# Expert layer of a two-block transformer: TensorE weighs a quad of tokens, and gives back its row places, two tiles sooner

## The chip, the cores and the metric

The kernel runs on one core of a Trainium2 chip. The time is that of one execution on the device, in microseconds (us); where several runs were made, it is their median. PE is TensorE, DVE is VectorE, ACT is ScalarE, POOL is GpSimd, SP is SyncE, whose queue issues the plain transfers.

## The reference

Two blocks follow each other on 256 tokens of width 1024: first two layers with attention or retention and a mixture of experts, then one layer that ends in `peer_ffn`. The change is in the last part alone:

```python
def peer_ffn(x, w_q, sub_k1, sub_k2, u_tab, v_tab):
    ...
    top_s, pos = lax.top_k(cand_s, PEER_TOPK)
    experts = jnp.take_along_axis(cand_i, pos, axis=-1)
    gates = jax.nn.softmax(top_s, axis=-1)
    ...
    def chunk(args):
        xc, ec, gc = args
        u = u_tab[ec].astype(f32)
        act = jax.nn.gelu(jnp.einsum('ced,cd->ce', u, xc.astype(f32))) * gc
        return jnp.einsum('ce,ced->cd', act, v_tab[ec].astype(f32)).astype(x.dtype)
```

Each token picks 128 of 16384 experts (8 heads, 16 each). An expert is a row `u` (a key, 1024 numbers) and a row `v` (a value). A token's output is the sum of its experts' values, each weighted by gelu(u.x) and its gate.

## The kernel before, in words

The stage `peer_stage` treats the 256 tokens in two halves, in two ways at once.

One half goes **by tiles**: all 16384 key rows are read in 128 tiles of 512 KB (`keys(n)`, n = 0 to 127), then all value rows in 128 more (`values(m)`, m = 0 to 127). SP's queue fetches them in this order into 6 places (and 13 spare ones for the first tiles); a place is fetched anew once PE has used the tile in it (`tile_used`).

The other half goes **by tokens**: POOL gathers the 128 rows of `u` and `v` that one token picked into one of 8 row places (1 MB each, `peer_rows_a`, `_b`, `_c`). A quad is four tokens. Two tokens make a pair p. `spread_pair(p)` on PE copies both tokens' x to all partitions (8 matmul rows); DVE's two `dot`s then multiply and sum; when a quad's four dots are done, ACT's `open_quad` applies the gelu and scales by the gates (four copies, semaphore `acted`). `values_of(q)`, called here the weighing of quad q, waits for `acted`, multiplies the four tokens' value rows (16 matmul rows at L3095) and signals `rows_used`. POOL waits for `rows_used` of quad q before it gathers the four tokens of quad q+2 into the places.

All of it shares the 16 DMA engines. PE, ACT, DVE and POOL each work in the order in which the code is written. That order has four parts: tiles 0 to 47, while DVE also picks the experts of the other half (`picks(0, ...)`, `recover(0, ...)`; the dots of pairs 0 to 7 stand between its steps; `PAIR_AT` says behind which tile a pair is spread: 19, 22, ... 40); then `turn_picks(0, 6)` and a wait for `selT_made`; then ten rounds of eight key tiles with three pairs each and, up to round eight, four gate units (L3107); then 128 value tiles with the remaining 26 pairs (`pairs_before`), one pair every four or five tiles. The end is a norm of both halves (from L3400) and the store.

Of the kernel before, what the change touches and what calls it, by code (L numbers as in the profile page):

```python
# [2859 lines left out]
PK = 128  # L2860
# [5 lines left out]
QUADS = P // QUAD  # L2866
# [10 lines left out]
PAIR_AT = {FIRST_TOKEN + 1 + 3 * p: p for p in range(BESIDE_PICKS // 2)}  # L2877
BESIDE_UNITS = 3 * GROUPS_LEFT
VALUES_FROM = BESIDE_PICKS + BESIDE_UNITS
# [81 lines left out]
def peer_stage(K, S, products, first, scores, room, out):  # L2961
# [28 lines left out]
    def pairs_before(m):  # L2990
        return VALUES_FROM // 2 + min(-(-m * ((TOKENS - VALUES_FROM) // 2) // (PK - 6)), (TOKENS - VALUES_FROM) // 2)

    with nc.Block() as block:  # L2993
# [22 lines left out]
        def _(pe):  # L3016
# [38 lines left out]
            def keys(n):  # L3055
                pe.wait_ge(tile_in[PLACE[n]], 16 * TURN[n])
                if n % 4 == 0 and n >= 8:
                    if n - 8 < EARLY:
                        pe.wait_ge(gelu_done, n // 4 - 1)
                    else:  # L3060
                        pe.wait_ge(tile_gated, (n - 8 - EARLY) // 4 + 1)
                u = first.slot(n).rearrange("p (k e) -> p k e", k=KD)
                for k in range(KD):
                    last = pe.matmul(K.bank[:, 2 + n // 4 % 2, n % 4 * P:(n % 4 + 1) * P], u[:, k, :], xT[:, k, :], start=(k == 0),  # L3064
                                     stop=(k == KD - 1))
                last.then_inc(tile_used, 1)
# [7 lines left out]
            def spread_pair(p):  # L3074
                if p:
                    pe.wait_ge(dotted, 2 * p)
                else:
                    pe.wait_ge(index_made, 1)
                for dh in range(2):
                    for n, part in enumerate(first.x_rows):  # L3080
                        for r in range(2):
                            t, own = token(2 * p + r), slice(64 * r, 64 * (r + 1))
                            last = pe.matmul(K.bank[:, 4 + 2 * r + dh, :], first.ident[own, t:t + 1].to_broadcast([64, P]),  # L3083
                                             part[own, dh * 512:(dh + 1) * 512], start=(n == 0), stop=(n == 1))
                last.then_inc(spread, 1)

            def weigh_pair(p):
                if p % 2 == 0 and p:
                    values_of(p // 2 - 1)

            def values_of(q):
                pe.wait_ge(acted, QUAD * (q + 1))
                for dh in range(2):
                    for g in range(QUAD):
                        last = pe.matmul(K.bank[32 * strip(g):32 * (strip(g) + 1), dh, :], W[:, q % 2, g, 31 - q:63 - q],  # L3095
                                         rows[(QUAD * q + g) % ROWS_HELD][:, D + dh * 512:D + (dh + 1) * 512], start=(q == 0),
                                         stop=(q == QUADS - 1))
                last.then_inc(rows_used, 1)

            def gate_unit(m):  # L3100
                pe.wait_ge(a_ready, m + 1)
                pe.wait_ge(b_ready, m + 1)
                pe.wait_ge(dotted, BESIDE_PICKS + 2 * (3 * (m // 4) + m % 4 // 2 + 1))
                if m >= 2:
                    pe.wait_ge(h_gated, m - 1)
                for q in range(QT):
                    last = pe.matmul(K.bank[:, 6 + m % 2, q * P:(q + 1) * P], a_hot[:, m % 2, q, :], b_hot[:, m % 2, q, :],  # L3107
                                     start=True, stop=True)
                last.then_inc(g_made, 1)

            def values(m):
                n = PK + m
                pe.wait_ge(tile_in[PLACE[n]], 16 * TURN[n])
                for dh in range(2):
                    last = pe.matmul(K.bank[:, 2 + dh, :], H[:, m, :], first.slot(n)[:, dh * 512:(dh + 1) * 512], start=(m == 0),  # L3115
                                     stop=(m == PK - 1))
                last.then_inc(tile_used, 1)
# [4 lines left out]
            for n in range(FIRST_TILES, EARLY):  # L3122
                keys(n)
                if n in PAIR_AT:
                    spread_pair(PAIR_AT[n])
                if n - 1 in PAIR_AT:
                    weigh_pair(PAIR_AT[n - 1])
            pe.wait_ge(dotted, BESIDE_PICKS)
            turn_picks(0, 6)
            pe.wait_ge(selT_made, 1)  # L3130
            for e in range(GROUPS_LEFT // 2):
                n, m, p = EARLY + 8 * e, 4 * e, BESIDE_PICKS // 2 + 3 * e
                spread_pair(p)
                keys(n)
                weigh_pair(p)
                keys(n + 1)
                if m < UNITS:
                    gate_unit(m)
                    gate_unit(m + 1)
                keys(n + 2)  # L3140
                pe.wait_ge(h_gated, min(m + 2, UNITS))
                spread_pair(p + 1)
                keys(n + 3)
                weigh_pair(p + 1)
                keys(n + 4)
                if m < UNITS:
                    gate_unit(m + 2)
                    gate_unit(m + 3)
                keys(n + 5)
                pe.wait_ge(h_gated, min(m + 4, UNITS))  # L3150
                spread_pair(p + 2)
                keys(n + 6)
                weigh_pair(p + 2)
                keys(n + 7)
            pe.wait_ge(h_gated, UNITS)
            pe.wait_ge(tile_gated, GROUPS_LEFT)
            for m in range(PK):
                for p in range(pairs_before(m), pairs_before(m + 1)):
                    spread_pair(p)
                values(m)  # L3160
                for p in range(pairs_before(m), pairs_before(m + 1)):
                    weigh_pair(p)
                if m == PK - 5:
                    values_of(QUADS - 1)

        @block.gpsimd
        def _(pool):
# [426 lines left out]
```

## Time and profile before

| | us |
|---|---|
| median of 3 runs (lowest, highest) | 1901.48 (1900.75, 1904.99) |
| the profiled execution, its time | 1908.66 |
| its span in the trace | 1906.8 |
| PE busy, share of the span | 1772.8, 93% |
| DVE, ACT, POOL busy | 905.9, 433.7, 431.5 |

Busy times of the whole span mix stages with different limits. The stage in question begins its key tiles at about 1228 us and takes the rest of the span. What ends a wait in each of its parts is told by the chain of work that ended last and by the GB/s that the DMA engines moved.

### The profile page before, as it was taken

To read this page: it belongs to the slowest core of one execution; us is meant where nothing else is said; L and a number is where in the kernel's file an instruction comes from. 1 tells how busy PE (TensorE), PEld (TensorE's weight loads), DVE (VectorE), ACT (ScalarE), POOL (GpSimd) and SP (SyncE) were. 2 spreads that over 40 slices of the span, in tenths; PEclk is the share of its full clock that TensorE was granted. 3 is DMA by queue.
4 is the path that set the end of the run, shared out by engine and by line. 5 is a ranking of instruction groups with operands and counts; after the bars stand their busy time and mean duration, and the time that the engine had idled before them with its cause. 6 is when DMAs were issued, how large, how long until landed. Compare 5 with 4: busy or idle time off the path is not lost. (4 is left out here: it accounts for less than half of the span.)

```text
span 1906.8 us, 23745 instructions
## 1 busy us (share of the span) xinstructions
PE 1772.8 (93%) x9356; PEld 1136.8 (60%) x9356; DVE 905.9 (48%) x1978; ACT 433.7 (23%) x847; POOL 431.5 (23%) x312
## 2 busy tenths in 40 slices
PE   4989999988999999998899999999999997999998
PEld 4975444436887754442586656988888874333333
DVE  4467311114477842111598743988776642211222
ACT  5462211114345321110330324311011110000001
POOL 5820000006667600000110004314222221121110
PEclk8999899998999989999999999999999999999999
DMA  9986899995567769999632335398999999999996
GB/s 395 354 324 213 326 430 429 429 430 194 198 245 286 270 253 429 430 428 429 259 122 99 120 131 218 133 383 333 402 414 415 415 416 410 388 407 403 403 401 248
DMA packets 95089, 620.29 MB, mean 325 GB/s; under 512 B 11520, under 2 KB 12032, under 8 KB 60672
## 3 DMA queue, kind: packets, MB, share of 16 engines
q1 hardware_dynamic: 75824, 482.88, 63.5%
q0 software_dynamic: 18432, 134.23, 17.3%
q8 instruction: 78, 1.28, 0.3%
q10 hardware_dynamic: 720, 1.61, 0.2%
q14 instruction: 35, 0.29, 0.0%
HBM read 617.63 MB, written 1.05 MB: 324 GB/s over the span
## 5 line engine op out<-in xcount | busy, mean ns | idle before, releaser
L3115 PE MATMUL bank<-peer_tiles_a,peer_H 128*128 128x512 f32 x344 | 159.7, 604 | 16.7 <-DMA peer_tiles_a<-in_peer_v 16.7
L232 POOL TENSOR_TENSOR w_lo<-ring,w_hi 128x1024 fp32r<-128x1024 f32 x60 | 148.1, 2471 | 64.5 <-ACT w_hi L222 64.1
L3322 DVE CUSTOM_DVE_ANT_0 peer_junk<-peer_rows_b,bank 128x1024 bf16<-128x1024 f32 x64 | 76.8, 1217 | 146.0 <-issue 138.7
L1096 PE MATMUL bank<-ring,moe_slots 128*64 128x512 f32 x576 | 131.4, 607 | 9.8 <-DMA ring<-in_stream 9.8
L3064 PEld LDWEIGHTS bank<-peer_xT,peer_tiles_a 128*128 128x128 f32 x1104 | 127.3, 192 | 21.4 <-issue 15.6
L3064 PE MATMUL bank<-peer_xT,peer_tiles_a 128*128 128x128 f32 x1104 | 135.2, 278 | 4.7 <-DMA peer_tiles_a<-in_peer_u 4.7
L3322 DVE CUSTOM_DVE_ANT_0 peer_junk<-peer_rows_a,bank 128x1024 bf16<-128x1024 f32 x48 | 57.4, 1218 | 146.7 <-issue 131.9
L3115 PEld LDWEIGHTS bank<-peer_tiles_a,peer_H 128*128 128x128 f32 x344 | 62.1, 189 | 105.5 <-issue 73.5
L3179 POOL DMA_INDIRECT peer_rows_b<-in_peer_uv,peer_index x64 | 60.0, 937 | 235.3 <-PE bank L3095 220.4
L3179 POOL DMA_INDIRECT peer_rows_a<-in_peer_uv,peer_index x48 | 48.2, 1003 | 264.5 <-PE bank L3095 218.6
L1277 DVE TENSOR_TENSOR bank<-bank,mod 128x512 f32<-128x512 f32 x32 | 22.4, 700 | 175.3 <-PE bank L1146 175.3
L1096 PE MATMUL bank<-early,moe_slots 128*64 128x512 f32 x448 | 102.0, 597 | 3.6 <-DMA early<-in_stream 3.6
L1146 PE MATMUL bank<-ring,moe_hidT 128*64 128x512 f32 x448 | 99.8, 595 | 3.8 <-issue 2.3
L339 DVE CUSTOM_DVE_ANT_0 mod<-sb_mod_ring,bank 128x1024 bf16<-128x1024 f32 x64 | 76.6, 1217 | 47.3 <-DMA sb_mod_ring<-in_ada_t 22.9
L1096 PEld LDWEIGHTS bank<-ring,moe_slots 128*64 128x64 f32 x576 | 43.0, 139 | 93.2 <-issue 76.1
L3221 ACT ACTIVATE peer_opened<-peer_pre 128x4 f32<-128x4 f32 x32 | 6.6, 206 | 386.6 <-DVE peer_pre L3322 377.5
L222 ACT ACTIVATE w_hi<-ring 128x1024 fp32r<-128x1024 f32 x60 | 63.6, 1060 | 108.8 <-PE bank L261 73.1
L3115 PE MATMUL bank<-peer_tiles_b,peer_H 128*128 128x512 f32 x168 | 79.2, 605 | 4.2 <-DMA peer_tiles_b<-in_peer_v 4.1
L3064 PEld LDWEIGHTS bank<-peer_xT,peer_tiles_b 128*128 128x128 f32 x544 | 64.8, 196 | 14.0 <-issue 12.7
L3064 PE MATMUL bank<-peer_xT,peer_tiles_b 128*128 128x128 f32 x544 | 70.2, 284 | 3.1 <-issue 2.9
L1465 POOL TENSOR_TENSOR w_lo<-ring,w_hi 128x1024 fp32r<-128x1024 f32 x4 | 9.5, 2417 | 280.6 <-ACT w_hi L1205 280.6
L1146 PEld LDWEIGHTS bank<-ring,moe_hidT 128*64 128x64 f32 x448 | 32.6, 137 | 63.7 <-issue 56.1
(515 smaller groups left out, 3684.0 us busy)
## 6 DMA issues: line engine op xcount, KB each, us to landing
ring<-in_stream SPq DMA_DIRECT2D x103, 2048.0 KB, 12.8
early<-in_stream SPq DMA_DIRECT2D x32, 2048.0 KB, 18.4
peer_tiles_a<-in_peer_v SPq DMA_DIRECT2D x86, 512.0 KB
peer_tiles_a<-in_peer_u SPq DMA_DIRECT2D x69, 512.0 KB
sb_mod_ring<-in_ada_t SPq DMA_DIRECT2D x64, 512.0 KB, 6.3
peer_tiles_b<-in_peer_v SPq DMA_DIRECT2D x42, 512.0 KB
peer_tiles_b<-in_peer_u SPq DMA_DIRECT2D x34, 512.0 KB
ret_mod_ring<-in_ada_t SPq DMA_DIRECT2D x32, 512.0 KB, 5.0
```

Of the source, the lines that this page charges most:

```text
L222: act.activation(self.shaped(self.w_hi, q, by_columns), self.quarter(n, q, by_columns), ACT.Copy).then_inc(self.hi_made, 1)
L232: pool.tensor_tensor(self.shaped(self.w_lo, q, by_columns), self.quarter(n, q, by_columns), self.shaped(self.w_hi, q, by_columns).bitcast( ...
L339: dve.tensor_tensor_reduce(out=self.junk[:, b % 2, :], in0=self.ring[:, b % self.slots, :], in1=c_wide, scale=1.0, scalar=0.0, op0=ALU.mul ...
L1096: last = pe.matmul(K.bank[own(e), 4 + up, :], slots[:, f, own(2 * p + e)], w[:, e, k, :], start=(f == 0), stop=(f == KD - 1))
L1146: last = pe.matmul(K.bank[own(e), 6 + dh, :], hidT[:, k, own(e)], w[:, e, k, :], start=(k == 0), stop=(k == 3))
L1277: dve.tensor_tensor(y, y, K.mod[:, 2 * D + dh * 512:2 * D + (dh + 1) * 512], ALU.mult).then_inc(y_gated, 1)
L1465: pool.tensor_tensor(next_shaped(w_lo, q), next_quarter(q), next_shaped(w_hi, q).bitcast(F32), ALU.subtract).then_inc(next_lo, 1)
L3064: last = pe.matmul(K.bank[:, 2 + n // 4 % 2, n % 4 * P:(n % 4 + 1) * P], u[:, k, :], xT[:, k, :], start=(k == 0), stop=(k == KD - 1))
L3115: last = pe.matmul(K.bank[:, 2 + dh, :], H[:, m, :], first.slot(n)[:, dh * 512:(dh + 1) * 512], start=(m == 0), stop=(m == PK - 1))
L3179: pool.indirect_dma_start(rows[i % ROWS_HELD], None, K.A["peer_uv"], bass.IndirectOffsetOnAxis(ap=index[:, token(i):token(i) + 1], axis=0) ...
L3221: act.activation(opened[:, q % 2, :], pre[:, q, :], ACT.Gelu_apprx_tanh).then_inc(quad_gelu, 1)
L3322: dve.tensor_tensor_reduce(out=junk[:, i % 2, :], in0=rows[i % ROWS_HELD][:, 0:D], in1=wide_row(i % 2), scale=1.0, scalar=0.0, op0=ALU.mul ...
```

## The change

A pair's call of `weigh_pair` now weighs the quad that the pair itself ends (p odd), where it weighed the quad ended by the pair before (p even). The calls stand elsewhere: in the first part two tiles behind the spread of the odd pair; in the rounds behind the gate units that follow two tiles later; among the value tiles behind the fourth tile from the spread, `weigh_pair(VALUES_FROM // 2 - 1)` behind the first one.

```diff
             def weigh_pair(p):
-                if p % 2 == 0 and p:
-                    values_of(p // 2 - 1)
+                if p % 2:
+                    values_of(p // 2)
...
-                if n - 1 in PAIR_AT:
-                    weigh_pair(PAIR_AT[n - 1])
+                if n - 2 in PAIR_AT:
+                    weigh_pair(PAIR_AT[n - 2])
...
                 spread_pair(p)
                 keys(n)
-                weigh_pair(p)
+                if e:
+                    weigh_pair(p - 1)
                 keys(n + 1)
                 if m < UNITS:
                     gate_unit(m)
                     gate_unit(m + 1)
+                weigh_pair(p)
                 keys(n + 2)
...
                 keys(n + 3)
-                weigh_pair(p + 1)
                 keys(n + 4)
                 if m < UNITS:
                     gate_unit(m + 2)
                     gate_unit(m + 3)
+                weigh_pair(p + 1)
                 keys(n + 5)
...
                 keys(n + 6)
-                weigh_pair(p + 2)
                 keys(n + 7)
...
                 values(m)
-                for p in range(pairs_before(m), pairs_before(m + 1)):
-                    weigh_pair(p)
-                if m == PK - 5:
-                    values_of(QUADS - 1)
+                if m == 0:
+                    weigh_pair(VALUES_FROM // 2 - 1)
+                if m >= 3:
+                    for p in range(pairs_before(m - 3), pairs_before(m - 2)):
+                        weigh_pair(p)
```

Three places of PE's order are shown. A key tile is 8 matmuls (L3064), a value tile 2 (L3115), a spread the four rows of L3083, a weighing the four rows of L3095.

**PE, first part, tiles 35 to 40, with the weighing of quad 2.** Before, from tile 35:

```order
L3064 MATMUL bank<-peer_xT,peer_tiles_b 128x128 x16
L3064 MATMUL bank<-peer_xT,peer_tiles_a 128x128 x8
L3083 MATMUL bank<-peer_x_rows_hi,peer_ident 128x512 x2
L3083 MATMUL bank<-peer_x_rows_lo,peer_ident 128x512 x2
L3083 MATMUL bank<-peer_x_rows_hi,peer_ident 128x512 x2
L3083 MATMUL bank<-peer_x_rows_lo,peer_ident 128x512 x2
L3064 MATMUL bank<-peer_xT,peer_tiles_a 128x128 x8
L3095 MATMUL bank<-peer_rows_a,peer_W 32x512 x3
L3095 MATMUL bank<-peer_rows_b,peer_W 32x512
L3095 MATMUL bank<-peer_rows_a,peer_W 32x512 x3
L3095 MATMUL bank<-peer_rows_b,peer_W 32x512
L3064 MATMUL bank<-peer_xT,peer_tiles_a 128x128 x16
```

With the change, from the same tile 35:

```order
L3064 MATMUL bank<-peer_xT,peer_tiles_b 128x128 x16
L3095 MATMUL bank<-peer_rows_a,peer_W 32x512 x3
L3095 MATMUL bank<-peer_rows_b,peer_W 32x512
L3095 MATMUL bank<-peer_rows_a,peer_W 32x512 x3
L3095 MATMUL bank<-peer_rows_b,peer_W 32x512
L3064 MATMUL bank<-peer_xT,peer_tiles_a 128x128 x8
L3083 MATMUL bank<-peer_x_rows_hi,peer_ident 128x512 x2
L3083 MATMUL bank<-peer_x_rows_lo,peer_ident 128x512 x2
L3083 MATMUL bank<-peer_x_rows_hi,peer_ident 128x512 x2
L3083 MATMUL bank<-peer_x_rows_lo,peer_ident 128x512 x2
L3064 MATMUL bank<-peer_xT,peer_tiles_a 128x128 x24
```

The weighing stood behind tile 38; it stands behind tile 36, ahead of tile 37 and ahead of the spread of pair 6.

**PE, end of the first part, with the weighing of quad 3.** Before, from tile 43 on (the 3 transposes of L3071 are `turn_picks`):

```order
L3064 MATMUL bank<-peer_xT,peer_tiles_a 128x128 x32
L3064 MATMUL bank<-peer_xT,peer_tiles_b 128x128 x8
L3071 MATMUL bank<-consts,peer_sel 128x128 x3
L3083 MATMUL bank<-peer_x_rows_hi,peer_ident 128x512 x2
L3083 MATMUL bank<-peer_x_rows_lo,peer_ident 128x512 x2
L3083 MATMUL bank<-peer_x_rows_hi,peer_ident 128x512 x2
L3083 MATMUL bank<-peer_x_rows_lo,peer_ident 128x512 x2
L3064 MATMUL bank<-peer_xT,peer_tiles_b 128x128 x8
L3095 MATMUL bank<-peer_rows_b,peer_W 32x512 x3
L3095 MATMUL bank<-peer_rows_c,peer_W 32x512
L3095 MATMUL bank<-peer_rows_b,peer_W 32x512 x3
L3095 MATMUL bank<-peer_rows_c,peer_W 32x512
```

With the change, from tile 41 on:

```order
L3064 MATMUL bank<-peer_xT,peer_tiles_b 128x128 x16
L3095 MATMUL bank<-peer_rows_b,peer_W 32x512 x3
L3095 MATMUL bank<-peer_rows_c,peer_W 32x512
L3095 MATMUL bank<-peer_rows_b,peer_W 32x512 x3
L3095 MATMUL bank<-peer_rows_c,peer_W 32x512
L3064 MATMUL bank<-peer_xT,peer_tiles_a 128x128 x32
L3064 MATMUL bank<-peer_xT,peer_tiles_b 128x128 x8
L3071 MATMUL bank<-consts,peer_sel 128x128 x3
L3083 MATMUL bank<-peer_x_rows_hi,peer_ident 128x512 x2
L3083 MATMUL bank<-peer_x_rows_lo,peer_ident 128x512 x2
L3083 MATMUL bank<-peer_x_rows_hi,peer_ident 128x512 x2
L3083 MATMUL bank<-peer_x_rows_lo,peer_ident 128x512 x2
```

The weighing stood behind tile 48, past the transposes and the spread of pair 8; it stands behind tile 42, ahead of tiles 43 to 47 and of the transposes.

**PE, the last value tiles, with the weighing of quad 31.** Before, from tile 117 on:

```order
L3115 MATMUL bank<-peer_tiles_b,peer_H 128x512 x4
L3115 MATMUL bank<-peer_tiles_a,peer_H 128x512 x8
L3115 MATMUL bank<-peer_tiles_b,peer_H 128x512 x2
L3095 MATMUL bank<-peer_rows_b,peer_W 32x512 x3
L3095 MATMUL bank<-peer_rows_c,peer_W 32x512
L3095 MATMUL bank<-peer_rows_b,peer_W 32x512 x3
L3095 MATMUL bank<-peer_rows_c,peer_W 32x512
L3115 MATMUL bank<-peer_tiles_b,peer_H 128x512 x2
L3115 MATMUL bank<-peer_tiles_a,peer_H 128x512 x6
```

With the change, also from tile 117 on:

```order
L3115 MATMUL bank<-peer_tiles_b,peer_H 128x512 x4
L3115 MATMUL bank<-peer_tiles_a,peer_H 128x512 x4
L3095 MATMUL bank<-peer_rows_b,peer_W 32x512 x3
L3095 MATMUL bank<-peer_rows_c,peer_W 32x512
L3095 MATMUL bank<-peer_rows_b,peer_W 32x512 x3
L3095 MATMUL bank<-peer_rows_c,peer_W 32x512
L3115 MATMUL bank<-peer_tiles_a,peer_H 128x512 x4
L3115 MATMUL bank<-peer_tiles_b,peer_H 128x512 x4
L3115 MATMUL bank<-peer_tiles_a,peer_H 128x512 x6
```

Four value tiles stood behind the last weighing; seven do. In the same way quad 29, the last whose places are gathered anew, was weighed behind value tile 103 and is weighed behind tile 101; quad 19 behind tile 9, and now 7.

## Rows read from the trace of the kernel before

**Rows 1.** The page: span, and DMA share in 40 slices.

```profile
span 1906.8 us, 23745 instructions
...
DMA  9986899995567769999632335398999999999996
```

**Rows 2.** Stretches of the stage: engines busy, granted clock, DMA share, GB/s.

```profile
core 0: us, PE busy (x) PEld busy (x) DVE busy (x) ACT busy (x) POOL busy (x), PEclk, DMA share, GB/s
1288.00:1308.00 20.00, 20.00 (x172) 16.16 (x165) 17.64 (x78) 2.25 (x7) 5.97 (x7) 1.00 0.66 246
1308.00:1328.00 20.00, 20.00 (x168) 16.73 (x167) 17.24 (x33) 5.01 (x10) 16.68 (x7) 1.00 0.98 387
...
1364.00:1372.00 8.00, 8.00 (x70) 7.43 (x69) 3.66 (x6) 1.64 (x6) 3.45 (x4) 1.00 0.92 350
1372.00:1618.00 246.00, 231.35 (x1812) 182.40 (x1811) 137.29 (x287) 24.95 (x88) 52.49 (x56) 1.00 1.02 415
1618.00:1630.00 12.00, 12.00 (x46) 4.77 (x45) 2.37 (x4) 0.00 (x0) 3.76 (x4) 1.00 0.82 285
1630.00:1848.00 218.00, 204.35 (x671) 82.33 (x673) 47.18 (x79) 10.56 (x50) 33.76 (x36) 1.00 1.01 408
```

**Rows 3.** Chain that ended last, around the first row places of values.

```profile
1597.66 17.54 DMA peer_tiles_a<-in_peer_v
...
1615.25 3.70 PE bank L3115 x8
1618.95 1.13 PE bank L3083 x8
1620.07 1.91 PE bank L3115 x4
1621.99 1.85 PE bank L3095 x16
```

**Rows 4.** The same chain, near its end.

```profile
1847.64 1.86 PE bank L3095 x16
...
1899.90 1.23 DVE x L3400
```

**Rows 5.** One value tile in PE's order of time, with its wait.

```profile
1866.71 1.98 PE L3115 MATMUL bank<-peer_tiles_b,peer_H 128*128 128x512 f32 x4 [0.66 <-DMA peer_tiles_b<-in_peer_v]
```

**Rows 6.** Instructions of PE in order of time, while picks are made.

```profile
1309.70 3.84 PE L3064 MATMUL bank<-peer_xT,peer_tiles_b 128*128 128x128 f32 x32
...
1315.25 0.49 PE L3083 MATMUL bank<-peer_x_rows_hi,peer_ident 64*128 64x512 f32 x2
...
1318.35 0.63 PE L3095 MATMUL bank<-peer_rows_a,peer_W 128*32 128x512 f32 x3
...
1328.77 7.31 PE L3064 MATMUL bank<-peer_xT,peer_tiles_a 128*128 128x128 f32 x64
...
1338.20 0.49 PE L3071 MATMUL bank<-consts,peer_sel 128*128 128x128 f32 x3
1339.34 0.50 PE L3083 MATMUL bank<-peer_x_rows_hi,peer_ident 64*128 64x512 f32 x2 [0.65 <-DVE peer_selT L3373]
...
1342.43 0.63 PE L3095 MATMUL bank<-peer_rows_b,peer_W 128*32 128x512 f32 x3
...
1354.64 2.02 PE L3107 MATMUL bank<-peer_scores 128*128 128x128 f32 x16
...
1361.49 0.63 PE L3095 MATMUL bank<-peer_rows_a,peer_W 128*32 128x512 f32 x3
```

**Rows 7.** Instructions of DVE in the same stretch.

```profile
1311.07 1.22 DVE L3322 CUSTOM_DVE_ANT_0 peer_junk<-peer_rows_a,bank 128x1024 bf16<-128x1024 f32 x1 [1.55 <-PE bank L3083]
...
1316.69 1.22 DVE L3322 CUSTOM_DVE_ANT_0 peer_junk<-peer_rows_b,bank 128x1024 bf16<-128x1024 f32 x1 [0.87 <-PE bank L3083]
```

**Rows 8.** Instructions of ACT in the same stretch.

```profile
1313.71 0.85 ACT L3229 ACTIVATE peer_W<-peer_opened,peer_gates 128x1 f32<-128x1 f32 x4
...
1329.87 0.85 ACT L3229 ACTIVATE peer_W<-peer_opened,peer_gates 128x1 f32<-128x1 f32 x4
```

## The prediction

> **What bounds the kernel now.** I read the page first: the 16 DMA engines are at 9 tenths in nearly every slice of the last third, with one gap before it [rows 1]. Then I cut the stage into stretches [rows 2]. From 1372 to 1618 us the DMA engines move 415 GB/s at a share of 1.02, while PE has 231.35 of 246 us busy: PE waits 14.7 us there, the DMA engines never. From 1630 to 1848 it is 408 GB/s. Here bytes decide. But there are holes: 246 GB/s from 1288 to 1308, 387 up to 1328, 350 around 1364 and 285 from 1618 to 1630. Against 415 these are 8.1, 1.3, 1.3 and 3.8 us of lost transfer time (length times the missing share). In a hole all 6 tile places are full or wait for PE, and the row places wait for a weighing. So three things decide in turn: the order on PE, DVE and ACT up to about 1364, then the DMA engines, and at the very end PE alone: from quad 29's weighing at 1847.64 to the last tile's end at 1899.90, 52.3 us [rows 4], PE waits only once, 0.66 us before the tile at 1866.71 [rows 5].
>
> A tile (512 KB) costs the DMA engines 1.26 us at 415 GB/s, a quad's gathers (4 x 1 MB) 10.1 us. On PE a key tile costs 1.83 us (four in 7.31 [rows 6]), a value tile 1.8 (two in 3.70, with a switch), a spread 1.13 and a weighing 1.85 [rows 3].
>
> **The change part by part.** No instruction is added or removed; most of the 32 weighings move. What counts is what stands behind each on PE (tiles, spreads, transposes) and on POOL (the gathers), and whether the wait for ACT's copies still has cover.
>
> *The first part: a new wait.* Before, quad 2 was weighed at 1318.35, while ACT's copies ended at 1313.71 + 0.85 = 1314.56: cover of 3.8 us. Quad 3 was weighed at 1342.43 against copies that ended at 1330.72: 11.7 us [rows 6, 8]. With the change this cover goes. The spread of pair 5 ends at 1309.70, where tile 35 starts; tiles 35 and 36 take 3.7 and end at 1313.4; the copies come at 1314.56: PE waits 1.2 us, weighs for 1.85, does tile 37 (1.9) and only then spreads pair 6 (1.13), which ends at 1319.5. It was spread at 1315.25, and its dot began at 1316.69, held by PE for the last 0.87 [rows 6, 7]. The dot now begins at about 1319.8, 3.1 us late. Quads 0 and 1 are moved likewise; by the same sum they make the spread of pair 5 itself 0.5 to 1.4 us late (estimate). So DVE is 3.4 to 4.5 us late from pair 6 on, and nothing between that dot and quad 3's copies waited for anybody else: the copies end at 1334.1 to 1335.2.
>
> PE has by then fallen less behind: tile 42 ends at about 1330.3 (it was 1328.77, where tile 43 starts). It waits about 4 us, weighs (1.85), and does tiles 43 to 47 (9.4 to the transposes before, 9.2 without the small wait in it): transposes at 1345.2 to 1346.3 for 1338.20. The spread of pair 8 followed them by 1.14 [rows 6]: now at 1346.3 to 1347.4, 7.0 to 8.1 late. A weighing (1.85) no longer follows, but the first gate unit, which waits for pair 8's dots, had that as cover; I take 0.6 us for it (estimate). PE comes to tile 49, and so to what follows, 7.0 - 1.85 + 0.6 = 5.8 to 8.1 - 1.85 + 0.6 = 6.9 us late. Queued behind the wait: tiles 43 to 47, so their places, so SP's next fetches.
>
> *What it gives back there.* Quad 4 is weighed behind the gate units that end at 1354.64 + 1.86 = 1356.5 instead of at 1361.49 [rows 6]. Late by the above that is 1362.3 to 1363.4 for a start; it was 1361.49. So the request for quad 6's rows comes 0.8 to 1.9 us later than before, I take the middle, **+1.4**, and at that moment PE has done two tiles fewer (52 for 54), so two fewer places were fetched anew: a debt of 2 x 1.26 = **+2.5 us** of transfer. Its other side is a bigger hole around 1364. From here to the value tiles the DMA engines decide, PE's 14.7 us of waiting absorb its own delay, and in the rounds the weighings that move keep their cover: two tiles and two gate units (3.7 + 1.86 = 5.5 us) lie between the spread's end and them, and from the end of pair 5's spread to its copies' end it was 1314.56 - 1309.70 = 4.9.
>
> *Quad 18 to quad 19.* Quad 18 keeps its place. Quad 19 was weighed at 1621.99 behind tile 9; it is now weighed behind tile 7, which arrives at 1615.25 and is done at 1617.1: 4.9 us sooner [rows 3]. Two tiles less are 2.5 us of transfer, and the hole of 3.8 us [rows 2] gives the rest: **-4.9**. From quad 19 to quad 29 there are 94 tiles before and after, with as many long gaps of ten tiles, and a burst of gathers stands alike to the tiles around it. So the small holes in 408 GB/s come again: **0**.
>
> *The end.* Behind quad 29's weighing stand two more value tiles (3.6) and the spread of pair 60 (1.13); the wait of 0.66 may vanish. PE decides there, so this is paid in full: +4.0 to +4.7, I take **+4.4**. The last weighing, three tiles sooner, gives nothing: what follows it waits for the last tile [rows 4].
>
> **Sum:** 1.4 + 2.5 - 4.9 + 4.4 = **+3.4 us**. The profiled execution took 1908.66 us for a span of 1906.8, 7.2 above the median; I put the difference onto both: 1912.1 in such a run, 1901.48 + 3.4 = **1904.9** as a median.
>
> *A rule against this sum.* The row shows one rate, 415 GB/s, with gathers and tiles in flight together [rows 2]. The Trainium skill, DMA: Bandwidth & Descriptors, section Issuing engines are not separate DMA queues, says that transfers from any engine end up on the same 16 DMA engines and interleave. By that rule an earlier request only changes whose bytes go first: the sum would be 0 and the time 1901.5. By the rows it is +3.4, as PE, not the DMA engines, holds both ends. The rate agrees with the rule in the middle.
>
> **The rivals.**
> - *Faster: the new wait costs nothing.* If DVE's late pair 6 is caught up (its steps to the next dots may have slack that the records do not show), +1.4 and +2.5 go. Earlier gathers of quads 2 to 5 then fill holes of the first stretch, up to 2.5 us of the 10.7 lost before 1372. 4.4 - 4.9 - 2.5 = -3.0: 1898.5. It decides once PE's waits for quads 2 and 3 together stay under 2 us. Against it: the copies of quad 3 lie 2 us behind tile 42 even with DVE's old times. Chance 0.2.
> - *Slower: the hole at 1618 only moves.* Tile 7 arrived with its neighbours in a bunch; if the gathers that come 4.9 us sooner meet them, the tiles behind are held up and quad 20 gains just the two tiles, 2.5. Then 1.4 + 2.5 - 2.5 + 4.4 = +5.8: 1907.3. For it: PE waited through a tile's 17.54 us there [rows 3]. Against it: 3.8 us in which little moved. Chance 0.2.
> - *No change: bytes alone decide.* The wait in the first part is paid from PE's 14.7 us and the end from tiles that come sooner: 1901.5, as by the rule above. Against it: the holes at both ends. Chance 0.15.
>
> **How the numbers follow.** The forecast keeps 0.45 with a range of its own of 1902.5 to 1907.5 (+0.8 or +1.9 for the first term, 4.0 or 4.7 for the last, and 1 us for rounding of holes). With the rivals' 1898.5 and 1907.3 and 1 to 1.5 us beside them for the median's own scatter, the range is 1897.5 to 1909. A measurement tells about 0.2%, 3.8 us, from no change: below 1897.7 lies half of the first rival and little else, 0.13; above 1905.3 lie nearly half of the forecast and most of the second, 0.38; the rest, 0.49, is the same within it.
>
> **What the profile after would show.** Right: PE waiting for ACT's copies ahead of L3095, 1 us for quad 2 and 3 to 5 us for quad 3; the transposes of the first part near 1345; a hole of 3 to 5 us near 1360 to 1366; none near 1618 and quad 19 weighed some 5 us sooner after quad 18; 56 to 57 us from quad 29's weighing to the last tile. Wrong: quad 3's weighing behind tile 42 with a wait under 1 us, or GB/s after 1372 that differ from 415 in the middle, since then the order of requests itself matters.

## The result: 6 us slower, about twice the forecast

| | before | after |
|---|---|---|
| median of 20 runs (lowest, highest) | 1903.02 us (1899.24, 1907.19) | 1908.97 us (1905.54, 1914.02) |
| ratio to before, 95% interval | | 1.0033 (1.0025 to 1.0042) |
| the profiled execution, its time | 1908.66 | 1910.28 |
| its span | 1906.8 | 1908.4 |

By the ratio the change costs 6.3 us (4.8 to 8.0) where the forecast had 3.4, and the sign is beyond doubt. The two profiled executions are only 1.6 us apart. The first thing to settle is therefore which of them stands for its kernel, and the trace of before does not. The page of after, against [rows 1]:

```profile
span 1908.4 us, 23745 instructions
...
DMA  9986899995568769999633335399899999999996
...
PE 24%; DMA 10%; DVE 3%; issue 1%; ACT 0%; DVEq 0%
```

It tells little: the same number of instructions, four of the 40 digits changed by one, and for the chain of work that ended last shares of PE and DMA only (the last line). So I read PE in order of time where the first waits were forecast. With [rows 6] beside it (in these rows a key tile is x16, a value tile x4 and a weighing x16):

```profile
1308.63 0.63 PE L3095 MATMUL bank<-peer_rows_a,peer_W 128*32 128x512 f32 x3 [0.16 <-ACT peer_W L3231]
...
1320.26 3.84 PE L3064 MATMUL bank<-peer_xT,peer_tiles_b 128*128 128x128 f32 x32
1327.96 1.08 PE L3095 MATMUL bank<-peer_rows_b,peer_W 128*32 128x512 f32 x3 [3.86 <-ACT peer_W L3231]
...
1331.54 8.55 PE L3064 MATMUL bank<-peer_xT,peer_tiles_a 128*128 128x128 f32 x64
...
1341.71 0.49 PE L3071 MATMUL bank<-consts,peer_sel 128*128 128x128 f32 x3
...
1348.61 1.58 PE L3107 MATMUL bank<-peer_scores 128*128 128x128 f32 x12 [0.78 <-DVE peer_pre L3324]
```

In front of quad 3's weighing PE stands still for 3.86 us, for ACT's copies. In front of quad 2's it is 0.16 us only, where I had 1.2. What I had not forecast comes behind the wait. One matmul of the weighing lasts 1.08 us instead of 0.63, the whole weighing takes 1331.54 - 1327.96 = 3.6 us instead of 1.85, and tiles 43 to 46 take 8.55 instead of 7.31. ACT's copies, as in [rows 8], end at 1327.06 + 0.85 = 1327.91:

```profile
1327.06 0.85 ACT L3231 ACTIVATE peer_W<-peer_opened,peer_gates 128x1 f32<-128x1 f32 x4
```

The stretches of after, with those of [rows 2] to compare (the last three columns are the granted clock, the DMA share and GB/s):

```profile
1272.00:1372.00 100.00, 94.20 (x761) 78.07 (x760) 77.96 (x213) 13.68 (x40) 28.07 (x21) 0.97 0.92 365
1324.00:1328.00 4.00, 0.14 (x5) 0.04 (x6) 3.97 (x6) 1.05 (x5) 0.00 (x0) 0.89 1.02 427
1328.00:1332.00 4.00, 4.00 (x18) 1.03 (x19) 3.93 (x3) 0.00 (x0) 0.09 (x1) 0.50 0.89 361
1332.00:1336.00 4.00, 4.00 (x29) 4.00 (x29) 2.42 (x4) 0.60 (x1) 3.08 (x4) 0.76 0.62 198
1350.00:1364.00 14.00, 14.00 (x118) 11.37 (x116) 11.92 (x29) 1.64 (x6) 2.36 (x2) 1.00 0.63 216
1372.00:1590.00 218.00, 211.22 (x1751) 175.20 (x1750) 133.48 (x280) 23.87 (x86) 53.12 (x52) 1.00 1.02 414
1618.00:1630.00 12.00, 7.82 (x16) 2.59 (x16) 2.17 (x4) 0.00 (x0) 1.61 (x2) 1.00 1.02 419
1630.00:1660.00 30.00, 26.82 (x89) 11.30 (x89) 7.11 (x12) 2.12 (x10) 3.74 (x4) 1.00 0.97 373
```

The granted clock is 0.50 from 1328 to 1332, the lower of the two levels (1.2 GHz), right behind 3.86 us in which PE did nothing. It is back at 1.00 (2.4 GHz) from 1336. The Trainium skill, TensorE: Matmul & The Clock Gate, section The HAM clock gate, says that the array falls to half its clock when it idles and gets it back once it is busy; the trace agrees. Two holes, stretches in which the DMA engines move much less than 415 GB/s, are seen in the last column: 198 GB/s from 1332 to 1336 and 216 from 1350 to 1364. From 1372 to 1590 it is 414, as before. The hole at 1618 is gone; one stands at 1630 to 1660.

The chain of work that ended last, near the end of after (start, us, what), as in [rows 4]:

```profile
1830.65 11.81 DMA peer_tiles_a<-in_peer_v
...
1844.49 1.85 PE bank L3095 x16
...
1853.04 10.52 DMA peer_tiles_a<-in_peer_v
...
1887.44 1.85 PE bank L3095 x16
1889.30 12.23 PE bank L3115 x28
1901.53 0.02 issue
1901.55 1.23 DVE x L3402
```

From quad 29's weighing it is 1901.53 - 1844.49 = 57.0 us to the last tile's end, with the seven tiles (12.23 us) behind the last weighing.

### The profile page after: what moved, and what is told of

It is laid out like the page before. It is cut to its first block and busy times, and to the rows that moved or that the text cites. A ratio compares the mean times of both kernels' runs of the same rounds, so it can differ in the third digit from the quotient of the medians.

```text
span 1908.4 us, 23745 instructions
## 1 busy us (share of the span) xinstructions
PE 1772.5 (93%) x9356; PEld 1136.5 (60%) x9356; DVE 908.3 (48%) x1978; ACT 433.1 (23%) x847; POOL 433.5 (23%) x312
## 5 line engine op out<-in xcount | busy, mean ns | idle before, releaser
L3115 PE MATMUL bank<-peer_tiles_a,peer_H 128*128 128x512 f32 x344 | 160.0, 604 | 17.2 <-DMA peer_tiles_a<-in_peer_v 17.2
L3064 PEld LDWEIGHTS bank<-peer_xT,peer_tiles_a 128*128 128x128 f32 x1104 | 128.2, 193 | 23.2 <-issue 16.1
L3064 PE MATMUL bank<-peer_xT,peer_tiles_a 128*128 128x128 f32 x1104 | 136.0, 280 | 4.9 <-DMA peer_tiles_a<-in_peer_u 4.9
L3115 PEld LDWEIGHTS bank<-peer_tiles_a,peer_H 128*128 128x128 f32 x344 | 62.1, 189 | 105.8 <-issue 73.9
L3115 PE MATMUL bank<-peer_tiles_b,peer_H 128*128 128x512 f32 x168 | 78.6, 603 | 2.5 <-DMA peer_tiles_b<-in_peer_v 2.5
L3064 PEld LDWEIGHTS bank<-peer_xT,peer_tiles_b 128*128 128x128 f32 x544 | 62.8, 192 | 11.9 <-issue 8.2
L3064 PE MATMUL bank<-peer_xT,peer_tiles_b 128*128 128x128 f32 x544 | 67.1, 279 | 2.7 <-DMA peer_tiles_b<-in_peer_u 2.7
## 6 DMA issues: line engine op xcount, KB each, us to landing
peer_tiles_a<-in_peer_u SPq DMA_DIRECT2D x69, 512.0 KB, 11.1
```

## The experiments

All kernels below but the one with a filler have the instructions of before. Where a weighing stands is written in tables, "behind tile n: quad q", so the line numbers differ a little (the weighing is L3093, a key tile L3066, a value tile L3113). Each ratio is to the kernel before on the same chip, in rounds; us are the ratio's distance from 1 times 1903. Intervals are 95%. Each kernel has one profiled execution, so what is read from traces rests on one execution each.

### The order of before, profiled once more

No edit but the tables with the old places (the second table, for the value tiles, is left out here):

```diff
+WEIGHED_FIRST = {26: 0, 32: 1, 38: 2}
```

> The order of before, profiled once more, since the profiled execution of before took 1908.66 us against a median of 1903.02 over 20 runs. Theory A (that execution lost some 5.5 us to a hiccup of PE ahead of the spread of pair 0, where PE's clock was 0.69 for 4 us, and everything behind it is late by that): a span near 1901, the spread of pair 0 some 5 us sooner, near 1265.5 as in the profile after. Theory B (the hiccup belongs to the order): it is there again, span near 1906.

It took 1903.1 us (span 1901.3), 5.6 less than the profiled execution of before. Nearly the whole difference lies ahead of pair 0's spread. In the trace of before, single matmuls of one tile stand apart there:

```profile
1261.62 0.36 PE L3064 MATMUL bank<-peer_xT,peer_tiles_b 128*128 128x128 f32 x1 [0.71 <-issue]
1262.33 0.27 PE L3064 MATMUL bank<-peer_xT,peer_tiles_b 128*128 128x128 f32 x1 [0.35 <-issue]
...
1264.46 4.90 PE L3064 MATMUL bank<-peer_xT,peer_tiles_b 128*128 128x128 f32 x27 [0.43 <-issue]
```

and as a stretch of the same kernel, the granted clock at 0.69:

```profile
1264.00:1268.00 4.00, 3.56 (x22) 3.54 (x22) 1.64 (x8) 0.60 (x1) 0.00 (x0) 0.69 1.03 431
```

Pair 0 is spread at 1271.08 in that execution and at 1265.92 in this one, 5.2 us sooner. So this trace, not the first, is the one to hold beside after; it is called "the order of before" from here on. Its stretches:

```profile
1272.00:1372.00 100.00, 99.17 (x829) 83.96 (x832) 84.04 (x229) 14.54 (x43) 30.17 (x21) 1.00 0.97 390
1350.00:1364.00 14.00, 14.00 (x118) 11.32 (x117) 9.47 (x21) 1.02 (x4) 3.75 (x4) 1.00 0.95 375
1372.00:1590.00 218.00, 210.98 (x1734) 172.44 (x1727) 130.25 (x270) 23.52 (x83) 48.97 (x53) 1.00 1.02 415
1618.00:1630.00 12.00, 12.00 (x36) 5.26 (x33) 2.37 (x4) 0.81 (x5) 3.76 (x4) 1.00 0.88 338
```

The loss of transfer time against 415 GB/s from 1272 to 1372 is 100 x (1 - 390/415) = 6.0 us here and 100 x (1 - 365/415) = 12.0 in after: 6.0 more, about the 6.3 of the ratio. (With the stretch laid from 20 to 120 us behind the first transposes of the picks in each execution, the rates change by 1 GB/s at most.)

### One part of the change at a time

```diff
 first: only the first part new
+WEIGHED_FIRST = {24: 0, 30: 1, 36: 2, 42: 3}
 rounds: only the rounds new (weighings behind the gate units)
 values: only the value tiles new
-WEIGHED_LAST = {0: 18, 9: 19, 18: 20, ... 93: 28, 103: 29, 112: 30, 123: 31}
+WEIGHED_LAST = {0: 18, 7: 19, 17: 20, ... 92: 28, 101: 29, 110: 30, 120: 31}
```

> Only the first part has the new order (quads 0 to 3 weighed behind tiles 24, 30, 36, 42); rounds and value tiles as before. Theory A (the first part holds the cost: PE's waits for ACT's copies, 3.9 us for quad 3 alone, and the slower clock behind that wait): slower by 4 to 7 us, ratio 1.002 to 1.004. Rival (the end holds it, the two tiles behind quad 29): within 1.5 us of before.

Measured: 1.0035 (1.0021 to 1.0049), +6.7 us (4.0 to 9.3). The first part alone costs what the whole change costs.

> Only the ten rounds have the new order; the first part and the value tiles as before. Theory A: the weighings keep their cover, quad 4 comes some 4.7 us sooner, the small hole near 1364 closes: 0 to 1.3 us faster, ratio 0.9993 to 1.0. Rival (requests that come sooner crowd out the tiles): slower by 1 to 3 us.

Measured: 0.9991 (0.9979 to 1.0002), -1.7 us (-4.0 to +0.4): a gain is not shown.

> Only the value tiles have the new order; first part and rounds as before. Theory A: quad 19 comes 4.9 us sooner and the end pays 4.8 us: within 1.5 us of before. Rival (the end holds the cost and the hole near 1618 only moves): slower by 3 to 5 us, ratio 1.0015 to 1.0026.

Measured: 0.9995 (0.9983 to 1.0006), -1.0 us (-3.2 to +1.1), where my sum had -4.9 + 4.4 = -0.5.

> The changed order in the rounds and among the value tiles, the first part as before. Theory A (the whole cost is in the first part): not slower, between -4 and 0 us against before, ratio 0.998 to 1.0. Rival (the later parts' own costs, the end above all, show once they are together): slower by 2 us or more.

Rounds and value tiles new, the first part old: 1.0001 (0.9993 to 1.0010), +0.2 us (-1.3 to +1.9). The whole change less this one is 6.3 - 0.2 = 6.1 us: the first part again.

### The first part: which quad, and the clock

```diff
 quads 0 to 2 only
+WEIGHED_FIRST = {24: 0, 30: 1, 36: 2}
 quad 3 only
+WEIGHED_FIRST = {26: 0, 32: 1, 38: 2, 42: 3}
```

> The order of before, but quads 0, 1 and 2 weighed behind tiles 24, 30 and 36, so ahead of the next pair's spread; quad 3 stays behind tile 48. Theory A (the cost of the first part is quad 3's wait of 3.9 us, with PE's slower clock behind it, on top of a DVE chain made some 3 us late by the spread of pair 6): transposes of the first part some 2.5 to 3 us late, no lower clock behind them, slower by 1 to 3 us, ratio 1.0005 to 1.0016. Rival (the late DVE chain alone is the cost): slower by 5 us or more.

Measured: 1.0007 (0.9997 to 1.0017), +1.3 us (-0.6 to +3.2). The clock stays at 1.00.

> The order of before, but quad 3 weighed behind tile 42 and not behind tile 48; quads 0 to 2 as before. Theory A: in the profile before, tile 42 ended 2 us ahead of the copies, so PE waits 2 us there and not 3.9; the transposes come 3.9 to 4.5 us late (2.0 of wait, 1.85 of weighing), of which 1.85 is given back behind the spread of pair 8: slower by 2 to 3 us, up to 5 if the clock falls behind this shorter wait too. Rival (quad 5's rows, asked for 9 us sooner, pay for it): same or faster.

Measured: 1.0000 (0.9990 to 1.0010), 0.0 us (-1.9 to +1.9), where 2 to 3 were expected. PE waits there too, but 1.69 us, and the clock stays up (the weighing takes 1.85 again):

```profile
1322.88 0.63 PE L3093 MATMUL bank<-peer_rows_b,peer_W 128*32 128x512 f32 x3 [1.69 <-ACT peer_W L3228]
...
1324.73 7.41 PE L3066 MATMUL bank<-peer_xT,peer_tiles_a 128*128 128x128 f32 x64
```

The stretch around it, with the granted clock third from the right:

```profile
1320.00:1340.00 20.00, 17.53 (x150) 15.02 (x148) 14.93 (x24) 2.25 (x7) 5.02 (x5) 1.00 1.02 418
```

By the medians the cost is more than the sum of its parts: +1.3 and 0.0 alone, +6.7 together. Quads 0 to 2 make DVE late and so ACT's copies; quad 3 makes PE wait for them. Only with both is the wait 3.86 us and the clock lost. The traces see less of a jump: each part alone loses 2.4 us more of transfer time than the order of before, both together 6.3 (the table further down). For quad 3 alone these 2.4 us do not show in the time, and why is open.

```diff
 first part new, and tile 42's eight matmuls issued three times (16 more)
-                for k in range(KD):
+                for k in list(range(KD)) * (3 if n == 42 else 1):
```

> As the run with only the first part changed, but PE computes tile 42 three times into the same place (16 more matmuls, 3.7 us), which fills its wait for quad 3's copies; the result is the same. Theory A (the clock falls because PE stood still): the granted clock between 1325 and 1340 us stays near 1, quad 3's weighing takes 1.85 us again, the transposes come 1.2 to 3 us sooner than in that run, and the time is 1 to 3 us below it. Rival (the clock has another reason, or the DMA engines decide by then): clock or time as in that run, or later, as tile 42's place is given back 3.7 us later.

Measured: 1.0026 (1.0017 to 1.0036), +4.9 us. The wait is filled with work, and the clock stays at 1.00:

```profile
1324.88 0.63 PE L3093 MATMUL bank<-peer_rows_b,peer_W 128*32 128x512 f32 x3 [0.29 <-ACT peer_W L3228]
...
1335.77 0.49 PE L3073 MATMUL bank<-consts,peer_sel 128*128 128x128 f32 x3
```

```profile
1320.00:1340.00 20.00, 19.06 (x166) 16.74 (x165) 14.90 (x22) 2.25 (x7) 4.76 (x4) 1.00 0.95 376
```

To compare executions I count from the first transposes of the picks (`consts,peer_sel`, at 1250.78 in after, 1251.15 in the order of before, 1247.67 here). The second transposes come 81.8 us later in the order of before, 90.9 in after and 88.1 here. So of after's 9.1 us of delay 6.3 are the wait and the order, 2.8 the clock. With the first part alone they come 89.4 us later, so the same wait cost only 1.3 us of clock in that execution. In time the filled kernel is 1.8 us better than the first part alone, but their intervals overlap (3.2 to 6.9 and 4.0 to 9.3); the share of the clock is read from the traces, not shown by the medians.

```diff
 the change, but quad 3 behind tile 45
+WEIGHED_FIRST = {24: 0, 30: 1, 36: 2, 45: 3}
```

> The changed order, but quad 3 weighed behind tile 45 and not 42; everything else as in the change. Theory A (the wait for quad 3's copies and the clock behind it are most of the cost): three tiles (5.5 us) cover the wait of 3.9, the clock stays, the transposes of the first part come some 6 us sooner than in the profile after, and the time is 4 to 6 us below the change, ratio 1.000 to 1.0015 against before. Rival (DVE, late by the spreads of pairs 2, 4 and 6, or the end decides): within 2 us of the change.

Measured: 1.0011 (0.9999 to 1.0024), +2.1 us (-0.2 to +4.6), for 5.9 (3.6 to 8.0) of the change on the same chip. Three tiles more ahead of quad 3 give the cover back: its weighing starts without a wait, clock 1.00.

```profile
1330.49 0.63 PE L3093 MATMUL bank<-peer_rows_b,peer_W 128*32 128x512 f32 x3
...
1336.02 0.49 PE L3073 MATMUL bank<-consts,peer_sel 128*128 128x128 f32 x3
```

### The end

```diff
 the last three weighings back where they were, the rest of the value tiles new
-101: 29, 110: 30, 120: 31
+103: 29, 112: 30, 123: 31
```

> The changed order itself, timed and profiled once more beside the next three on the same chip: ratio near 1.0033. In the profile, if PE's clock falls because of its long wait for quad 3's copies, as in the two profiles with that wait so far, it is under 1 between 1320 and 1340 us again; if that was chance, it is 1.

The change itself again, on the chip of this group: 1.0031 (1.0019 to 1.0042), +5.9 us, span 1906.6. The clock fell again: 0.83 as the mean of 1320 to 1340 us.

> The changed order, but quads 29, 30 and 31 weighed behind value tiles 103, 112 and 123, as before. Theory A (PE decides behind quad 29, and two tiles and a spread more stand there in the change): 4.7 us less from quad 29's weighing to the last tile, which itself comes 2.5 us (two tiles of transfer) later: 2.2 us below the change, ratio near 1.002. Rival (the DMA engines decide there too, so quad 29's later rows cost what the shorter end gives): as the change, within 1 us.

The old end, with the change elsewhere: 1.0053 (1.0033 to 1.0072), +10 us. My sum counts the end at +4.4, so all of it should have come back, and 2.2 us less than the change was expected; there is no gain at all. Its chain, with the same two waits for tiles as in after:

```profile
1833.31 11.80 DMA peer_tiles_a<-in_peer_v
...
1851.88 1.85 PE bank L3093 x16
...
1859.12 12.46 DMA peer_tiles_b<-in_peer_v
...
1897.72 7.08 PE bank L3113 x16
```

From quad 29's weighing to the last tile it is 1904.80 - 1851.88 = 52.9 us, shorter by 4.1 as reckoned. But quad 29 is weighed 7.4 us later than in after: the tile waited for lands 2.6 us later (1845.10 for 1842.46; quad 28, up to which the two kernels are the same, is already 2.7 late, so that is the execution, not the edit), and the two tiles and the spread now stand ahead of the weighing, 4.8 us. What is taken away behind is put in front. The second wait, behind quad 29, ends 1871.58 - 1845.10 = 26.5 us behind the first where it was 1863.56 - 1842.46 = 21.1. That it is 4 us slower than the change (its interval, 6.3 to 13.7 us, overlaps that of the change, 3.6 to 8.0) is not shown; that the old end gives nothing back is.

> The first part and quads 29 to 31 as before, the changed order in the rounds and for quads 19 to 28: what is left of the change when both costly ends are undone. Theory A: 2 to 4 us faster than before, ratio 0.998 to 0.999. Rival (an earlier request in the middle gives nothing, as the bytes decide there): same as before, ratio 0.9995 to 1.0005.

With the first part old: 1.0005 (0.9993 to 1.0017), +1.0 us (-1.3 to +3.2), where 2 to 4 us of gain were expected: that expectation failed. No kernel of these is shown to beat before; the nearest is the rounds alone.

## Why the prediction was right or wrong

| kernel | quad 3's wait | clock 1320 to 1340 | quad 4 | GB/s 1272 to 1372 | loss against 415 | time |
|---|---|---|---|---|---|---|
| order of before | none | 1.00 | 105.1 | 390 | 6.0 | 0 |
| quad 3 only | 1.69 | 1.00 | 107.7 | 380 | 8.4 | 0.0 |
| quads 0 to 2 only | none | 1.00 | 107.5 | 380 | 8.4 | +1.3 |
| first part, filled | 0.29 | 1.00 | 110.4 | 369 | 11.1 | +4.9 |
| first part | 3.87 | 0.91 | 111.7 | 364 | 12.3 | +6.7 |
| rounds only * | none | 1.00 | 100.0 | 392 | 5.5 | -1.7 |
| all but the first part * | none | 1.00 | 100.5 | 393 | 5.3 | +0.2 |
| quad 3 behind 45 * | none | 1.00 | 102.9 | 387 | 6.7 | +2.1 |
| after * | 3.86 | 0.83 | 108.3 | 365 | 12.0 | +6.3 |
| after again * | 3.86 | 0.83 | 107.9 | 366 | 11.8 | +5.9 |

"Quad 4" is the time from the first transposes to quad 4's weighing. In the kernels with a star the rounds are new, so it stands two tiles sooner.

**Right: the mechanism of the first part.** A wait of about 4 us for quad 3 (3.86), the gate unit's wait (0.78 for 0.6), quad 4 weighed later instead of sooner, a hole near 1360, 415 GB/s from there on: all seen. The hole was larger than the 3 to 5 us forecast: 14 x (1 - 216/415) = 6.7 us from 1350 to 1364. The rival "the new wait costs nothing" would have had a sum under 2 us; it was 4.0. "Bytes alone decide" is wrong at this end: at 365 GB/s the DMA engines had room, and it was PE that held the places. Where they are full they move 414 GB/s in after and 415 in the order of before, whatever the order of the requests. That agrees with what the Trainium skill, DMA: Bandwidth & Descriptors, section Issuing engines are not separate DMA queues, says of transfers that interleave on the same 16 engines; the interleaving itself is seen in no run here.

**Wrong: the size of the first term.** I had +1.4 for quad 4's request and +2.5 for the debt of two tiles, 3.9; the whole change less the rest measured 6.1. The step that failed is "It waits about 4 us, weighs (1.85), and does tiles 43 to 47 (9.4 to the transposes before ...)". It puts the work behind the wait at the full clock, so the clock at nothing. From the start of quad 3's weighing to the second transposes it takes 1335.77 - 1324.88 = 10.9 us with the wait filled and 1341.71 - 1327.96 = 13.8 in after (13.3 in after again, 13.6 with the old end, 12.2 with the first part alone). So the lost clock costs 1.3 to 2.9 us, 2.9 in the trace of after (2.8 if counted from the first transposes).

Another error went the other way. The waits for quads 0 to 2 were too large in the forecast (0.16 to 0.18 for 1.2 and 0.5 to 1.4), as they came from the stall in the first trace. ACT's copies of quad 2 begin at 1307.38 in the order of before and at 1313.71 in [rows 8], 6.33 us sooner, but PE's weighing of quad 2 at 1313.18 for 1318.35, only 5.17 sooner: in the disturbed execution the copies were 1.2 us late against PE, the whole of my 1.2. DVE was 2.9 us late with quad 3's copies (76.28 for 73.40 from the first transposes), for 3.4 to 4.5.

Together: from the first transposes on, quad 4 is weighed 1356.28 - 1251.15 = 105.1 us later in the order of before and 1359.10 - 1250.78 = 108.3 in after, 3.2 late for my 1.4. Without the 2.9 us of clock it would be 0.3 late (an estimate). With the debt that is 3.2 + 2.5 = 5.7 of the 6.0 us of extra loss in the table.

**Wrong: what the later parts give back.** My 3.9 is itself a difference. By its own steps PE is 5.8 to 6.9 us late at tile 49, and quad 4's new place in the rounds gives back 1361.49 - 1356.5 = 5.0 less the debt of 2.5. So for the first part alone the same steps say +5.8 to +6.9, and +6.7 was measured, quad 4 weighed 111.7 - 105.1 = 6.6 late. (With the wait filled it is 5.3 late: the clock made up for the small waits that I had too large.) For the rounds alone they say -2.5, with the value tiles -3.0, and here the runs have -1.7 (-4.0 to +0.4) and +0.2 (-1.3 to +1.9): the second excludes the -3.0. Quad 4 is indeed weighed 5.1 and 4.6 us sooner in these two traces, but the loss only falls from 6.0 to 5.5 and 5.3. In the order of before the DMA engines run at 387 GB/s from 1350 to 1372, which leaves 22 x (1 - 387/415) = 1.5 us to win there; that this is the reason is argued, not shown. So the miss of 6.3 - 3.4 = 2.9 us has two candidates. By the traces the first term is 1.8 us too small: the clock's 2.9, less what the small waits had too much. By the medians 3.2 us that should have come back did not. How the two share the miss, the runs do not say.

**Where PE weighs**, in us (the first transposes, the quads' weighings, the last tile's end):

| | first transposes | quad 3 | quad 4 | quad 18 | quad 19 | quad 29 | last tile |
|---|---|---|---|---|---|---|---|
| order of before | 1251.15 | 1337.21 | 1356.28 | 1587.52 | 1616.51 | 1841.95 | 1894.35 |
| after | 1250.78 | 1327.96 | 1359.10 | 1597.31 | 1612.70 | 1844.42 | 1901.53 |

**Right in sum, by luck: the value tiles.** -0.5 forecast, -1.0 (-3.2 to +1.1) measured. But none of its three terms stood, and two runs exclude the pair -4.9 and +4.4. Rounds and value tiles new with the old end should have given -2.5 - 4.9 = -7.4 and measured +1.0 (-1.3 to +3.2). The change with the old end should have given 3.4 - 4.4 = -1.0 and measured +10 (+6.3 to +13.7).

In after's trace quad 18, late by another 7.0 us, came back by 13.6 up to quad 19 (-4.9 forecast). The 7.0 belongs to the new rounds: from quad 4 to quad 18 it is 242.1 us with the rounds alone and 241.4 with all but the first part, for 231.2 in the order of before and 238.2 in after. The hole did not close but moved behind quad 19: 12 x (1 - 338/415) = 2.2 us at 1618 in the order of before, 30 x (1 - 373/415) = 3.0 at 1630 in after. That is the second rival's mechanism; quads 19 to 29 then took 6.3 us more for my 0. And the end was +4.7 in the trace for my 4.4 (by the chains, 57.0 us for 1894.35 - 1842.02 = 52.3), yet taking it back gives nothing, because quad 29's place sets both what stands behind it and when it comes: the term was counted from the weighing, and ought to have been counted from the wait for a tile ahead of it. Nor was the end PE's alone, as I had read from [rows 4]. The chain of the order of before holds a tile's transfer behind quad 29 (and so does that of [rows 4], 11.79 us from 1854.87, in the part left out there):

```profile
1849.25 11.88 DMA peer_tiles_b<-in_peer_v
```

This transfer began once PE had done three tiles behind the weighing, and PE then waited 0.65 us for it, so the end hangs on the transfers too.

The second rival's time, 1907.3, is nearer to the measured one than mine, but for a cost in the value tiles that was not there.

**The base.** Of the 4.1 us between my median, 1904.9, and the measured one, 1.5 is the base: the median of 3 runs was 1901.48, that of 20 is 1903.02. I had put the 7.2 us between the profiled execution and the median onto both. Most of it was a stall of PE at 1261 to 1268 with a lower clock behind it, which no other trace here shows: noise, as taken. But my stretches 1288 to 1328 of [rows 2] were read from behind that stall, and 246 GB/s for 348 made the first part look as if it had a hole of 8.1 us to give. This execution loses 11.1 us up to 1372, 5.1 more than the order of before profiled again, and is 5.6 us slower: loss and time go together here as in after.

**Open.** How much of the 6.3 us is the clock and how much the order is not told apart by the medians (4.9 us with the wait filled, 3.2 to 6.9, against 6.7, 4.0 to 9.3). Why quad 18 comes later with the new rounds and why 13.6 us come back up to quad 19 is not explained: no run moves quad 18's neighbours alone, and the trace with the old end is 2.7 us later at quad 28 than after, though both have the same order up to there. "Quad 3 behind 45" costs 2.1 us with hardly more loss than before (6.7); its interval touches 0.

## What to carry to other kernels

Work that is moved forward in one queue must be checked against the time at which its inputs will be ready after the move: here two small shifts, +1.3 and 0.0 us alone, made one long wait together, +6.7. Where the DMA engines are full behind a place, the loss against the full rate ahead of it is a good number to compare. The four kernels of the table that lost 5.1 to 6.3 us more than the order of before were slower by 4.9 to 6.7 us. But a loss of 2.4 us more did not show in the time of one kernel, and the change with the old end, which loses as much as after, was slower by 10. The other way gave nothing measurable: requests that came some 5 us sooner, where hardly a hole was left, did not shorten the time. A wait of the matmul engine counted at its own length is too little when it is some us long; the work behind it has to be costed at the lower clock. A term must also be counted from the wait ahead of it, not from the instruction that moves. And profile the kernel before twice before reading holes from one execution.

## What the runs showed of the hardware

- After 3.86 us without work PE ran at a granted clock of 0.50 (1328 to 1332) and then 0.76, and was at 1.00 from 1336; after 1.69 us without work it stayed at 1.00. The same wait gave 0.83 three times (after, after again, the old end) and 0.91 once (the first part alone) as the mean of 1320 to 1340.
- In the last key tiles and among the value tiles PE often waits 1.7 to 1.8 us for a tile, and the clock stays at 1.00 behind these waits. Twice it fell there too: to 0.63 in the 4 us behind a wait of 2.04 us that followed one of 1.78 (all but the first part, 1632.13), and to 0.60 behind one of 1.92 (rounds alone, 1766.98).
- With sixteen matmuls that only repeat a tile in place of the same wait the clock stayed at 1.00, and the work behind it was 2.9 us shorter than in after and 1.3 shorter than with the first part alone.
- Key tiles and gathers together ran at 413 to 415 GB/s from 1372 to 1590 in all traces, whatever the order of the requests.
